# RWKV chunk matrices from 64-row tiles, states block-diagonal by head, level masks on the products

## What is computed

```python
P  = rmsnorm(x) @ w_in                    # [RWKV-7 | MLA | gates]
A  = RWKV-7 time mixing                   # 16 heads of 64
B  = latent attention, chunk-causal       # 8 heads
x  = x + (sigmoid(Ga) * A + sigmoid(Gb) * B) @ w_out
x  = x + ConvGLU(rmsnorm(x))              # D_FF 5632
```

```python
def step(S, inp):
    r_t, w_t, k_t, v_t, kk_t, a_t = inp
    sa = einsum('bhvk,bhk->bhv', S, kk_t)
    S = S * w_t + v_t k_t^T - sa (kk_t * a_t)^T
    return S, einsum('bhvk,bhk->bhv', S, r_t)
```

## Time and profile before

| | |
|---|---|
| median of three runs | 2730.82 us |
| profiled execution | 2726.28 us |
| its span | 2724.4 us |
| PE busy | 2600.8 us, 95% |
| DVE busy | 1210.6 us, 44% |
| ACT busy | 858.6 us, 32% |
| POOL busy | 184.5 us, 7% |
| RWKV stage | about 100 to 870 us |
| mean granted TensorE clock | 0.982 |

### The profile page before, as it was taken

How to read it: one execution, slowest core, us unless ns; L and a number is a source line. 1 busy time by engine, 2 the same in 40 slices (tenths; PEclk the granted TensorE clock), 3 DMA queues, 4 the chain that set the end, 5 groups by cost and what they waited for, 6 DMA issues and landing times.

```text
span 2724.4 us, 40698 instructions
## 1 busy us (share of the span) xinstructions
PE 2600.8 (95%) x15484; PEld 2398.5 (88%) x15484; DVE 1210.6 (44%) x1916; ACT 858.6 (32%) x1244; POOL 184.5 (7%) x222
## 2 busy tenths in 40 slices
PE   6999999999999999999999979999999999999997
PEld 6879778877888899999997779999987899999885
DVE  4555555565454333324443354444423344444233
ACT  4322322322132333224432243333322233333232
POOL 3111201110110101000000000000000000000010
PEclk9999999999999999999999989999999999999998
DMA  5322111211114334333444324444343444444443
GB/s 164 86 59 60 48 54 46 65 43 57 53 52 99 118 100 121 94 88 108 131 124 168 124 78 126 128 123 128 119 128 125 125 123 129 125 124 130 140 129 118
DMA packets 414062, 283.41 MB, mean 104 GB/s; under 512 B 31680, under 2 KB 392642, under 8 KB 412720
## 3 DMA queue, kind: packets, MB, share of 16 engines
q1 hardware_dynamic: 405168, 259.16, 32.2%
q0 software_dynamic: 8832, 23.36, 2.9%
HBM read 275.55 MB, written 6.92 MB: 104 GB/s over the span
## 4 chain that ended last, share of the span: by engine, by line
PE 87%; DVE 8%; issue 2%; ACT 2%; DMA 1%; DVEq 0%; POOL 0%; SPq 0%; ACTq 0%; POOLq 0%
PE banks L1275 18%; PE banks L733 16%; PE banks L735 16%; PE banks L734 16%; PE banks L409 2%; PE banks L419 2%; PE banks L744 2%; PE banks L745 2%; PE banks L746 2%; PE banks L417 2%; PE banks L314 1%; PE banks L426 1%; DVE t_y L630 1%; DVE x_lo L803 1%; DVE w_lo L723 1%
## 5 line engine op out<-in xcount | busy, mean ns | idle before, releaser
L723 DVE TENSOR_TENSOR w_lo<-w_raw,w_hi 128x1024 fp32r<-128x1024 f32 x482 | 590.5, 1225 | 1061.6 <-ACT w_hi L718 1054.8
L733 PE MATMUL banks<-x_hi,w_hi 128*128 128x384 f32 x2640 | 918.7, 348 | 7.9 <-DVE w_lo L723 5.0
L735 PE MATMUL banks<-x_hi,w_lo 128*128 128x384 f32 x2640 | 891.8, 338 | 0.0
L734 PE MATMUL banks<-x_lo,w_hi 128*128 128x384 f32 x2640 | 891.6, 338 | 0.0
L718 ACT ACTIVATE w_hi<-w_raw 128x1024 fp32r<-128x1024 f32 x482 | 511.3, 1061 | 1046.7 <-PE banks L735 613.2
L733 PEld LDWEIGHTS banks<-x_hi,w_hi 128*128 128x128 f32 x2640 | 502.5, 190 | 19.3 <-issue 7.1
L734 PEld LDWEIGHTS banks<-x_lo,w_hi 128*128 128x128 f32 x2640 | 503.2, 191 | 2.7
L735 PEld LDWEIGHTS banks<-x_hi,w_lo 128*128 128x128 f32 x2640 | 501.9, 190 | 0.0
L1275 PE MATMUL banks<-w_hi,act_hi 128*128 128x512 f32 x528 | 164.8, 393 | 4.6 <-DVE h_rows L1790 2.4
L1275 PE MATMUL banks<-w_lo,act_hi 128*128 128x512 f32 x528 | 164.9, 394 | 0.0
L1275 PE MATMUL banks<-w_hi,act_lo 128*128 128x512 f32 x528 | 163.6, 391 | 0.0
(11 more groups left out here) (397 smaller groups left out, 2818.8 us busy)
## 6 DMA issues: line engine op xcount, KB each, us to landing
w_raw<-in_w_ffn_in SPq DMA_DIRECT2D x176, 512.0 KB, 3.9
w_raw<-in_w_in SPq DMA_DIRECT2D x144, 512.0 KB, 3.8
w_raw<-in_w_ffn_down SPq DMA_DIRECT2D x88, 512.0 KB, 3.4
w_raw<-in_w_out SPq DMA_DIRECT2D x32, 512.0 KB, 3.6
w_raw<-in_w_o_a SPq DMA_DIRECT2D x16, 512.0 KB, 4.0
w_raw<-in_w_o_b SPq DMA_DIRECT2D x16, 512.0 KB, 4.0
w_raw<-in_w_in SPq DMA_DIRECT2D x20, 256.0 KB, 3.8
w_ukv_head<-in_w_ukv POOLq DMA_DIRECT2D x8, 512.0 KB, 4.1
```

The source lines that it names most:

```text
L723: nc.vector.tensor_tensor(lo[:, s], raw[:, s], hi[:, s].bitcast(F32), ALU.subtract).then_inc(lo_done, 1)
L733: nc.tensor.matmul(out, hi[:, s, k, :], xh[:, kt, :], start=kt == 0, stop=False)
L734: nc.tensor.matmul(out, hi[:, s, k, :], xl[:, kt, :], start=False, stop=False)
L735: last = nc.tensor.matmul(out, lo[:, s, k, :], xh[:, kt, :], start=False, stop=kt == 15)
```

## The change

- **Products by 64-row tiles.** `al` and `rh` lose the zero planes, and each is made in one operation. The products of alpha and rho take only a head's 64 partitions of both operands, for head 0 and head 1 in turn. Results of head i go to bank b+i.
- **Head and tile as own dimensions.** The matrices are [P, 2, 3, P]; one DVE operation masks all six, by a mask row laid out as tile, tile, sample tile.
- **Level masks on the products.** POOL's level masks go. n_t itself is multiplied by t_x, and the transposed level mask is put on the product as it is copied to t_g, on DVE instead of ACT.
- **t_x by transposing t_y.** PE transposes t_y (after the identity) and ACT copies it; the mask nl1t goes. One piece of projection moves from behind the transposes to before them.
- **t_x before t_y.** The corrections of t_x and t_y have their own semaphore steps; a level's first product waits for t_x alone.
- **States block-diagonal.** `stb` [P, P] and `s0b` [P, 8, P] hold each head's state on the diagonal, zeros elsewhere. One product of 128 by 128 takes the place of two by head: in L382, L443, L469 and L484. They are written in two operations, one for each half of the partitions.

```diff
@@ pe_rwkv
             pe.wait_ge(E("s0_done"), f + 1)
-            for i in range(2):
-                for b in range(NB):
-                    last = mm_(ps[heads(i), 5, 16 * b:16 * b + 16], s0t[:, b, :],
-                               al[:, i, 256 + 16 * b:272 + 16 * b], start=True, stop=True)
+            for b in range(NB):
+                last = mm_(ps[:, 5, 16 * b:16 * b + 16], s0b[:, b, :], al[:, 256 + 16 * b:272 + 16 * b],
+                           start=True, stop=True)
...
-            for u in range(6):
-                last = mm_(unit(6, u), be[:, unit_tok(u)], al[:, unit_head(u), unit_tok(u)], start=True, stop=True)
+            for i, t in units(0):
+                last = mm_(head_tile(6, i, t), be[heads(i), tile_tok(t)], al[heads(i), tile_tok(t)],
+                           start=True, stop=True)
             last.then_inc(E("nt_ps"), 1)
...
             pieces(1)
-            pe.wait_ge(E("nt_done"), f + 1)
-            for u in range(6):
-                last = transpose(unit(2, u), n_t[:, u, :])
-            last.then_inc(E("n_ps"), 1)
-            pieces(3)
+            pieces(1)
+            pe.wait_ge(E("t_y_first"), f + 1)
+            for i, t in units(0):
+                last = transpose(head_tile(2, i, t), t_y[:, i, t, :])
+            last.then_inc(E("t_x_ps"), 1)
+            pieces(2)
             for lv in range(5):
-                pe.wait_ge(E("n_level_done"), f * 5 + (lv + 1))
                 if lv == 0:
                     pe.wait_ge(E("t_first_done"), f + 1)
                 else:
-                    pe.wait_ge(E("t_done"), f * 5 + lv)
-                for u in units(lv):
-                    last = mm_(unit(g_bank(lv), u), (c_k, c_b)[lv % 2][:, u, :], t_x[:, u, :], start=True, stop=True)
+                    pe.wait_ge(E("t_done"), f * 9 + (2 * lv - 1))
+                for i, t in units(lv):
+                    last = mm_(head_tile(g_bank(lv), i, t), n_t[:, i, t, :], t_x[:, i, t, :], start=True, stop=True)
                 last.then_inc(E("g_ps"), 1)
                 pieces(1)
                 pe.wait_ge(E("g_done"), f * 5 + (lv + 1))
                 if lv == 0:
                     pe.wait_ge(E("mt_done"), f + 1)
+                else:
+                    pe.wait_ge(E("t_done"), f * 9 + 2 * lv)
...
@@ chunk steps
+                if c:
+                    mm_(ps[r0:r0 + 64, 2, 0:P], al[:, cols], stb[:, :], start=True, stop=False,
+                        skip_group_check=True)
                 for i in range(2):
-                    last = mm_(ps[r0:r0 + 64, 2, heads(i)], m_t[:, 2 * i + t, cs], v[:, t, heads(i)],
-                               start=True, stop=c == 0)
-                    if c:
-                        last = mm_(ps[r0:r0 + 64, 2, heads(i)], al[:, i, cols], st[:, 1, :], start=False, stop=True)
+                    last = mm_(ps[r0:r0 + 64, 2, heads(i)], m_t[:, i, t, cs], v[:, t, heads(i)],
+                               start=c == 0, stop=True, skip_group_check=True)
...
                 for i in range(2):
                     mm_(gain[i], tok[r0:r0 + 64, 0, t, heads(i)], v[r0:r0 + 64, t, heads(i)], start=True, stop=False)
-                    mm_(yo[i], v[:, t, heads(i)], c_k[:, 2 * i + t, cs], start=True, stop=False)
-                    if c:
-                        mm_(yo[i], st[:, 1, :], rh[:, i, cols], start=False, stop=False)
+                    mm_(yo[i], v[:, t, heads(i)], c_k[:, i, t, cs], start=True, stop=False, skip_group_check=True)
+                if c:
+                    mm_(ps[:, 5, cols], stb[:, :], rh[:, cols], start=False, stop=False, skip_group_check=True)
                 pe.wait_ge(E("u_done"), f * 4 + (c + 1))
...
-                        for b in range(NB):
-                            last = mm_(ps[heads(i), 5, 256 + 16 * b:272 + 16 * b], s0t[:, b, :],
-                                       rh[:, i, 256 + 16 * b:272 + 16 * b], start=False, stop=b == NB - 1,
-                                       skip_group_check=True)
+                    for b in range(NB):
+                        last = mm_(ps[:, 5, 256 + 16 * b:272 + 16 * b], s0b[:, b, :], rh[:, 256 + 16 * b:272 + 16 * b],
+                                   start=False, stop=b == NB - 1, skip_group_check=True)
@@ act_rwkv
-            fn(s0t[:, :, :], ps[:, 7, :].rearrange("p (b v) -> p b v", b=NB), ACT.Copy).then_inc(E("s0_done"), 1)
+            for i in range(2):
+                last = fn(s0b[heads(i), :, heads(i)], ps[heads(i), 7, :].rearrange("p (b v) -> p b v", b=NB), ACT.Copy)
+            last.then_inc(E("s0_done"), 1)
...
+            act.wait_ge(E("t_x_ps"), f + 1)
+            fn(t_x[:, :, :, :], head_tiles(2, 3), ACT.Copy).then_inc(E("t_first_done"), 1)
             for lv in range(5):
-                act.wait_ge(E("g_ps"), f * 5 + (lv + 1))
-                n = len(units(lv))
-                fn(t_g[:, 0:n, :], pair(g_bank(lv)).rearrange("p (u c) -> p u c", u=6)[:, 0:n, :], ACT.Copy)\
-                    .then_inc(E("g_done"), 1)
@@ dve_rwkv
-            link(tt(t_y[:, :, :], n_t[:, :, :], bc(cm["nl1"], 6), M))
-            link(tt(t_y[:, :, :], t_y[:, :, :], bc(ident, 6), A))
-            dve.wait_ge(E("n_ps"), f + 1)
-            link(masked(t_x, 2, (cm["nl1t"], cm["nl1t"])))
-            tt(t_x[:, :, :], t_x[:, :, :], bc(ident, 6), A).then_inc(E("t_first_done"), 1)
+            link(tt(n_t[:, :, :, :], head_tiles(6, 3), M_S, M))
+            link(tt(t_y[:, :, :, :], n_t[:, :, :, :], bc(cm["nl1"], 3), M))
+            tt(t_y[:, :, :, :], t_y[:, :, :, :], bc(ident, 3), A).then_inc(E("t_y_first"), 1)
...
             for lv in range(5):
+                n = tiles(lv)
+                dve.wait_ge(E("g_ps"), f * 5 + (lv + 1))
+                tt(t_g[:, :, 0:n, :], head_tiles(g_bank(lv), n), bc(cm[LEVELS[lv]], n), M).then_inc(E("g_done"), 1)
                 if lv in (0, 1, 3):
                     cut((3, 4, 0, 5)[lv])
...
-            link(tt(s0t[:, :, :], s0t[:, :, :], p3(6), A))
+            for i in range(2):
+                h = heads(i)
+                last = tt(s0t[h, :, :], s0b[h, :, h], p3(6)[h], A)
+            link(last)
@@ POOL, rwkv
-                pool.wait_ge(sem("nt_done"), f + 1)
-                for lv, name in enumerate(LEVELS):
-                    if lv >= 2:
-                        pool.wait_ge(sem("g_ps"), f * 5 + (lv - 1))
-                    n_u = len(units(lv))
-                    nc.gpsimd.tensor_tensor((c_k, c_b)[lv % 2][:, 0:n_u, :], n_t[:, 0:n_u, :], bc(cm[name], n_u),
-                                            ALU.mult).then_inc(sem("n_level_done"), 1)
```

125 lines of the change are left out of this document (63 added, 62 removed).

## The result

The changed kernel takes 2745.26 us (median of 20 runs, 2731.05 to 2756.01), the kernel before 2726.65 beside it (20 runs, 2722.97 to 2734.83): a ratio of 1.0065, interval 1.0051 to 1.0079. It is slower by 0.65%; the forecast was 2725. The profiled execution of after took 2740.97 us.

The account below looks back on a forecast made before the run. PE, busy 95%, was taken to bound the kernel, with DVE ending most stalls. Gains of 1.25, 0.66, 0.91 less losses of 1.17, 0.18, 0.07, 0.70 made 0.70 us per pass, 5.6 over eight: median 2725 us, range 2714 to 2737.

Parts of the forecast that it names:

- Part A: From the masked n_t to the first level product: DVE's chain gets shorter, 1.25 us gained per pass.
- Part B: The five levels: later masked copy on DVE, but no wait for t_y before the next level; 0.66 us gained per pass.
- Part C: The C products up to the first chunk product: 3.96 us becomes 3.05 with row tiles side by side, 0.91 gained per pass.
- Part D: The chunk steps: losses per pass of 1.17 us (wide state products), 0.18 (state halves on DVE) and 0.07 (step 0).
- the term of 0.39: Chunk steps 1 to 3: two changes of tile shape and a lost overlap cost 0.39 us each, 1.17 per pass.
- The 0.18 for the two halves of the state on DVE: Chunk steps: writing the by-head state in two halves takes 0.09 us longer, PE waits in two steps, 0.18 lost.
- Part E: DVE's tail: the sum into s0_t becomes two half-height operations of 0.68 us each, 0.70 lost per pass.
- rival (2): Longer waits before t_y's transposes and at L501 bring a second clock fall, 1.7 us per pass: 2739 us; chance 0.15.
- (1): Row tiles of nt, mt and C run one after the other, 1.15 to 1.25 us per pass gone: 2735 us; chance 0.13.
- (3): Chunk steps' shape changes hide in DVE's part of the ping-pong, state halves too, 1.35 us per pass back: 2714; chance 0.13.
- (4): Products cost by their count, so step 0 saves 0.93 us per pass: 2718 us; chance 0.05.

Follow-up runs that it names:

- e6: The changed kernel with the state products of chunk steps 1 to 3 by head again, step 0 still wide: 2699.66 us, 0.9894 of before.
- e1: The changed kernel with only step 0's start-state products by head again, 16 with 64 stationary columns: 2703.62 us, 0.9910 of before.
- e4: The changed kernel with DVE's tail as before: one add of 128 partitions, a third copy on ACT: 2729.84 us, 1.0005 of before.
- e2: The changed kernel with step 0's wide products moving 64 columns instead of 16, into an unused place: 2710.96 us, 0.9934 of before.
- e8: The kernel before with its start-state products (step 0 and alpha) made wide, 128 stationary and 16 moving columns: 2755.15 us, 1.0102 of before.
- e16: The changed kernel with steps 1 to 3 by head, step 0 wide, and the rk product issued twice: 2713.44 us, 0.9944 of before.
- e17: The changed kernel with steps 1 to 3 by head, step 0 wide, and the rk product issued three times: 2726.63 us, 0.9992 of before.
- e18: The kernel before with only the kk product (sum of squared keys) issued twice: 2716.23 us, 0.9960 of before.
- e15: The changed kernel with all state products by head, one add in DVE's tail and the kk product issued twice: 2687.86 us, 0.9849 of before.
- e7: The changed kernel with the 64-row products of nt, mt and C issued head 0 first, then head 1: 2741.18 us, 1.0041 of before.

## Why the prediction was wrong

The forecast of faster by 0.2% was wrong in sign, and the result lies above its range. Part by part:

- **Part A** said 1.25 us gained, measured 1.39 (7.18 to 5.79). The identity takes 0.96 without POOL beside it, as taken, and the nt and mt products run in pairs: 24 instructions in 1.54 us (212.77 to the piece at 214.31).
- **Part B** said 0.66, measured 0.69. The second product starts 0.17 late at the wide levels (222.56, 0.17 for the step of a piece, 222.90), as charged.
- **Part C** said 0.91, measured 1.10.
- **Part D** said 1.42 lost, measured 1.21: the four steps, from one's first product to the next one's, went from 7.34, 4.65, 4.87 and 4.70 to 7.62, 5.14, 5.15 and 4.86. The wide state products cost 0.37 to 0.39 a step (e6), which is the term of 0.39. The 0.18 for the two halves of the state on DVE don't show: with by-head products the steps take 4.78, 4.77 and 4.47 us, near or under the old ones. Step 0 lost 0.28 (7.34 to 7.62), not 0.07: its wide products cost 0.48 against the same by head (e1, 7.14), and the rest of the change gave 0.20 back. That the total is near is in part luck, since these two errors go against each other.
- **Part E** said 0.70 lost, measured 0.70 (2.61 to 3.31), with L511 waiting 1.26 as forecast (1.27); e4 gives it back.

The sum was 0.70 a pass and the measured terms make 1.27: at equal clock the change would win 10 us by this estimate, more than forecast. **The step that failed is the clock.** The sum priced every edit by its duration and took the granted clock as given; rival (2) allowed for a second fall, but looked for it behind two waits (before t_y's transposes and at L501) and at 1.7 us a pass, with 0.15. Neither wait brought one. The six new falls of 3.4 us near the second begin within 0.6 us of L506, before PE waits for L511, and behind a wait of 0.67 us that both kernels have; e4 has four of them with L511's wait back at 0.57. What brings these is open; they cost next to nothing. The main fall came where PE never waits, in the wide 16-column products of step 0, the edit that part D had put at 0.07 us, and it costs up to 5.7 us in a pass, 25.5 over all. It belongs to these wide products: e1 and e2 take it away by a change to them alone, and e8 brings it into the old kernel. The wide products of steps 1 to 3 bring none, but go with the longest.

Of the other rivals, (1) is refuted (tiles run side by side, even in the wrong order). (3) is refuted in its main part: the changes of shape don't hide; its small part, the state halves, did. (4) is refuted: 16 instructions with 128 stationary columns take 1.89 us, and 31 with 64 take 1.60 in e1 (259.54 to 261.14), so the time does not go by the count. Nor does it go by so few moving columns: 16 with 64 of them take 1.93 (e2). The Trainium skill, "TensorE: Matmul & The Clock Gate", section "LDWEIGHTS (loading the stationary operand)", says that a weight load's time goes by its columns and not by the contraction size; with so short a moving side these rows agree, 0.12 us for 128 columns and 0.05 for 64.

**Open:** whether a pass falls is tied here to the passes' spacing (e6 against e16 and e17), but no run tells what the chip looks at, nor why one pass falls for 3.4 us and the next for 13.7. The alpha products of L385, wide in the same way, stay wide in e1 and e2, which have no fall in the chunk steps. No run makes them by head alone; they stand between long products, and no fall starts there in any of these traces.

## What to carry to other kernels

Halving the number of products by making the stationary side wider saved no PE time here, where few columns move (1.89 us for half as many instructions as take 1.60), and PE moved fewer columns in that time: with such a group, look at the granted clock of the stretch in the profile of after, and try the narrow form. Before a term of a few hundred nanoseconds is trusted, ask whether the edit sits near a place where the clock could fall, since one fall of 13.7 us cost 5.7 us, ten times as much. And if one variant has a clean clock, move it by half a microsecond before believing the cause: here seven clean passes out of eight were due to their spacing.

## What the runs showed of the hardware

- The granted clock fell to 1.2 GHz with PE busy without a gap (13.65 of 13.65 us, clock 0.50), from the middle of 16 instructions of 128 stationary and 16 moving columns, in six of eight passes; with 64 moving columns, in the same time, in none of eight (e2).
- Useless products in a wait paid: 6.5 us of them gained 13.6 (e18).
- The spread between executions of one kernel goes with the clock: after ran from 2731 us at a mean clock of 0.972 to 2756 at 0.961, e15, with few falls, from 2685 to 2689.
- Tiles of the two row halves overlapped in fp32 (24 instructions in 1.54 us), and did so even when issued head after head, 0.32 us a pass worse than alternating (e7).
- A DVE operation of 768 columns took 2.47 us beside one of POOL and 0.96 without.
